# Block two's attention in a two-block layer kernel: where the softmax coefficients are applied, and which operand of p·v stands still

## The reference, cut to what matters

```python
s_c = jnp.einsum('bsgrd,bngd->bgrsn', qh, kc) - slopes * dist_c        # 15 compressed keys
p_c = masked_softmax(s_c, dist_c >= 0)
o_cmp = jnp.einsum('bgrsn,bngd->bsgrd', p_c, vc)
...
s = jnp.einsum('bgrqk,...', qb, kg) - slopes * dist                    # "selected", then "window"
pr = masked_softmax(s, valid)
o_slc = pr @ vg                                                        # o_win likewise
...
gates = jax.nn.sigmoid(gate).reshape(B, S, G, R, 3)
o = gates[..., 0:1] * o_cmp + gates[..., 1:2] * o_slc + gates[..., 2:3] * o_win
...
mixed = (g_a * (ya @ w_a2d) + g_b * (yb @ w_b2d)) @ w_o
```

## Time and profile before

| what | value |
|---|---|
| median of three runs | 1124.86 us |
| span of the profiled execution | 1122.6 us |
| PE busy | 1094.1 us (97%) |
| POOL busy | 902.3 us (80%) |
| ACT busy | 621.2 us (55%) |
| DVE busy | 495.1 us (44%) |
| mean granted clock of TensorE | 0.998 |

### The profile page before, as it was taken

How to read it: one execution, slowest core, us unless ns; L and a number is a source line. 1 busy time by engine, 2 the same in 40 slices (tenths; PEclk the granted TensorE clock), 3 DMA queues, 4 the chain that set the end, 5 groups by cost and what they waited for, 6 DMA issues and landing times.

```text
span 1122.6 us, 22288 instructions
## 1 busy us (share of the span) xinstructions
PE 1094.1 (97%) x8110; PEld 1023.2 (91%) x8110; DVE 495.1 (44%) x904; ACT 621.2 (55%) x1002; POOL 902.3 (80%) x695
## 2 busy tenths in 40 slices
PE   8999999999999999999999999999999999999997
PEld 7999998999998998999999899889999798999985
DVE  4422113202456554421126655774766256454463
ACT  4444444654667866544443775555666565555564
POOL 6999996898664596999999589577355898999985
PEclk9999999999999999999999999999999999999999
DMA  7866665666342454766665466335233565666652
GB/s 244 282 204 193 187 195 165 206 222 192 115 131 78 130 184 139 230 202 198 192 182 181 135 193 188 118 116 159 65 94 127 183 202 172 180 197 187 189 184 77
DMA packets 52774, 191.29 MB, mean 170 GB/s; under 512 B 5856, under 2 KB 6112, under 8 KB 52320
## 3 DMA queue, kind: packets, MB, share of 16 engines
q1 hardware_dynamic: 50688, 182.47, 52.6%
q10 hardware_dynamic: 2016, 7.81, 2.1%
HBM read 189.21 MB, written 1.05 MB: 169 GB/s over the span
## 4 chain that ended last, share of the span: by engine, by line
POOL 51%; issue 27%; PE 19%; ACT 1%; POOLq 1%; DVE 1%; DMA 1%; SPq 0%; DVEq 0%; ACTq 0%
POOL weights_low L533 51%; PE banks L575 10%; PE acc L575 8%; DMA ring<-in_stream 1%; POOLq L539 0%; ACT weights_high L1440 0%; POOLq L530 0%; ACT tmp L1686 0%; ACT tmp L1956 0%; PE acc L749 0%; PE banks L766 0%; DVE act_buf L2016 0%; DVE res L2162 0%; POOL stat L547 0%; DVE xs L2174 0%
## 5 line engine op out<-in xcount | busy, mean ns | idle before, releaser
L533 POOL TENSOR_TENSOR weights_low<-ring,weights_high 128x512 fp32r<-128x512 f32 x686 | 899.2, 1345 | 208.7 <-ACT weights_high L1440 206.5
L1440 ACT CAST weights_high<-ring 128x1024 fp32r<-128x1024 f32 x343 | 356.1, 1047 | 216.4 <-PE banks L575 132.0
L575 PE MATMUL banks<-xT_high,weights_high 128*128 128x256 f32 x1264 | 351.5, 278 | 1.2 <-POOL weights_low L533 1.1
L575 PE MATMUL banks<-xT_low,weights_high 128*128 128x256 f32 x1264 | 350.3, 277 | 0.0
L575 PE MATMUL banks<-xT_high,weights_low 128*128 128x256 f32 x1264 | 350.3, 277 | 0.0
L575 PEld LDWEIGHTS banks<-xT_high,weights_high 128*128 128x128 f32 x1264 | 237.4, 188 | 4.2 <-issue 1.5
L575 PEld LDWEIGHTS banks<-xT_low,weights_high 128*128 128x128 f32 x1264 | 237.7, 188 | 2.3
L575 PEld LDWEIGHTS banks<-xT_high,weights_low 128*128 128x128 f32 x1264 | 237.9, 188 | 0.0
L1991 DVE TENSOR_TENSOR hf<-act_buf,banks 128x256 f32<-128x256 f32 x40 | 16.8, 421 | 225.2 <-ACT act_buf L1466 211.0
L575 PE MATMUL acc<-xT_high,weights_high 128*128 128x256 f32 x408 | 108.8, 287 | 1.8 <-ACT xT_high L1539 1.0
L575 PE MATMUL acc<-weights_high,hT_high 128*128 128x512 f32 x264 | 104.0, 394 | 2.2 <-issue 1.6
(11 more groups left out here) (362 smaller groups left out, 1577.5 us busy)
## 6 DMA issues: line engine op xcount, KB each, us to landing
ring<-in_stream SPq DMA_DIRECT2D x343, 512.0 KB, 3.7
rows<-in_big_rows ACTq DMA_DIRECT2D x3, 1024.0 KB, 8.2
rows<-in_big_rows ACTq DMA_DIRECT2D x3, 512.0 KB, 4.0
cst<-in_consts ACTq DMA_DIRECT2D x3, 470.5 KB, 4.8
xs<-in_x_tm ACTq DMA_DIRECT2D x2, 512.0 KB, 7.3
out<-xs SPq DMA_DIRECT2D x4, 256.0 KB, 2.1
gates<-in_x_fm SPq DMA_DIRECT2D x2, 256.0 KB, 4.2
ring<-in_stream SPq DMA_DIRECT2D x2, 256.0 KB, 4.3
```

The source lines that it names most:

```text
L533: last = nc.gpsimd.tensor_tensor(wlo[:, slot, hs], ring[:, slot, hs], whi[:, slot, hs].bitcast(F32), ALU.subtract)
L575: ins = nc.tensor.matmul(o, lhsT, rhs, start=start, stop=stop, **kw)
L1440: nc.scalar.copy(whi[:, ch % RING, :], ring[:, ch % RING, :]).then_inc(S["hi_ready"], 1)
```

## The change

The coefficient (one over the row sum, times the gate) is now applied to the probabilities before they are transposed, for all three branches. The products can then be summed in PSUM, with features on partitions and tokens on columns, which is the layout `yT` needs. `both_tile(p)` is the half bank in which head pair p gathers compressed, selected and window products.

- `cmp_values` has v standing still (128 columns, two heads) and the probabilities moving; `both_values` has v of 64 columns standing still and 256 and 128 columns of probabilities moving, with m = 0 into the lower and m = 1 into the upper 64 partitions.
- DVE gets a multiply of 128x256 for each `tok` (signal `cmp_scaled`) and, in `both_coefs`, four multiplies in place on `both_prob` (128 and 256 columns, signal `both_scaled`). `both_coefs(h-1)` now stands ahead of `both_bias(h)`.
- `compressed_out`, `both_add`, `o2`, `turn_y(2)` and `turn_y(3)` are gone. `high_both` on ACT and `low_both` on DVE split a finished head pair (128x256) straight from PSUM. DVE's three multiplies on GDN's output move from rounds 1, 2, 3 to rounds 1, 3, 5.

```diff
+        def both_tile(p):
+
+            return acc[:, 2 + p % 2, T * (p // 2):T * (p // 2) + T]
...
                 for tok in range(2):
-                    pe.wait_ge(S["cmp_probs"], tok + 1)
+                    pe.wait_ge(S["cmp_scaled"], tok + 1)
...
                     pe.wait_ge(S["cmp_pt"], tok + 1)
-                    for g in range(2):
-                        last = nc.tensor.matmul(acc[:, 2 + tok, g * T:(g + 1) * T], cpT[:, tok, g * P:(g + 1) * P], bdv[:, g, :],
-                                                start=True, stop=True)
-                    last.then_inc(S["cmp_done"], 1)
+                    for p in range(4):
+                        g, heads = p // 2, slice(P * (p % 2), P * (p % 2) + P)
+                        mm(both_tile(p)[:, P * tok:P * tok + P], bdv[:, g, heads], cpT[:, tok, g * P:(g + 1) * P], tok == 0 and p < 2, False,
+                           skip_group_check=True)
...
-                src = og if k < 2 else o2
...
                     for tok in range(2):
-                        f = 2 * (k % 2) + kk
-                        last = nc.tensor.transpose(acc[:, (k + 2) % 4, (2 * kk + tok) * P:(2 * kk + tok + 1) * P],
-                                                   src[:, tok, f * P:(f + 1) * P], ident)
+                        f = 2 * k + kk
+                        last = nc.tensor.transpose(acc[:, k, (2 * kk + tok) * P:(2 * kk + tok + 1) * P],
+                                                   og[:, tok, f * P:(f + 1) * P], ident)
...
                 skip(f"both_t{e}")
-                pe.wait_ge(S["both_probs"], 4 * e + 4)
+                pe.wait_ge(S["both_scaled"], e + 1)
...
                 pe.wait_ge(S["both_pt"], e + 1)
-                if e >= 2:
-                    pe.wait_ge(S["both_out"], e - 1)
-                vc = P * (e % 2) + 64 * (e // 4)
-                for m in range(2):
-                    pT, o = both_pT[:, e % 2, m], acc[:, e % 2, P * m:P * m + P]
-                    mm(o[:, 0:64], pT[:, 0:P], sm[:, 0, vc:vc + 64], True, True)
-                    mm(o[:, 64:P], pT[:, P:2 * P], sm[:, 0, vc:vc + 64], True, False)
-                    last = mm(o[:, 64:P], pT[:, 2 * P:3 * P], sm[:, 1, vc:vc + 64], False, True)
+                p, kind = e // 2, e % 2
+                if p >= 2 and kind == 0:
+                    pe.wait_ge(S["yT_ready"], p - 1)
+                vc = P * kind + 64 * (e // 4)
+                two = [(both_tile(p)[64 * m:64 * m + 64], both_pT[:, kind, m]) for m in range(2)]
+                for o, pT in two:
+                    mm(o, sm[:, 0, vc:vc + 64], pT[:, 0:T], False, False, skip_group_check=True)
+                for o, pT in two:
+                    last = mm(o[:, P:T], sm[:, 1, vc:vc + 64], pT[:, T:3 * P], False, kind == 1, skip_group_check=True)
...
                     if h in (1, 2):
-                        pe.wait_ge(S["cmp_out"], h)
+                        pe.wait_ge(S["cmp_pt"], h)
...
                     if b == 0 and k % 2 == 0:
-                        pe.wait_ge(S["yT_ready"], k // 2 + 1)
+                        pe.wait_ge(S["yT_ready"], 2 + k // 2 + 1)
+                    if b == 1 and k >= 2:
+                        pe.wait_ge(S["yT_ready"], 2 + k + 1)
...
             done(mix_part(o[1], 0))
-            pe.wait_ge(S["both_out"], H2)
-            turn_y(2)
-            turn_y(3)
             mix_part(o[2], 0)
-            pe.wait_ge(S["yT_ready"], 4)
...
-            def high_y(k, order):
-                act.wait_ge(S["yT_turned"], order + 1)
-                nc.scalar.copy(yT[0][:, 2 * k:2 * k + 2, :].rearrange("p a t -> p (a t)"), acc[:, (k + 2) % 4, :]
+            def high_y(k):
+                act.wait_ge(S["yT_turned"], k + 1)
+                nc.scalar.copy(yT[0][:, 2 * k:2 * k + 2, :].rearrange("p a t -> p (a t)"), acc[:, k, :]
                                ).then_inc(S["yT_high"], 1)
+            def high_both(p):
+                wait_job(f"both_o{2 * p + 1}")
+                nc.scalar.copy(yT[0][:, 4 + p, :], both_tile(p)).then_inc(S["yT_high"], 1)
...
                     both_copy(h - 1)
+                if h in (4, 6):
+                    high_both(h // 2 - 2)
...
             both_exp(H2 - 1)
-            high_y(0, 0)
-            high_y(1, 1)
+            high_y(0)
+            high_y(1)
+            high_both(2)
...
             act.wait_ge(S["gmix_raw"], 16)
-            high_y(2, 2)
-            high_y(3, 3)
+            high_both(3)
...
                     link(v.tensor_scalar(cc, cc, c("rowvalid"), None, ALU.mult))
+                v.tensor_tensor(s3, s3, cc.unsqueeze(2).broadcast_to([P, H2, 32]), ALU.mult).then_inc(S["cmp_scaled"], 1)
...
-            def compressed_out(tok):
-                dve.wait_ge(S["cmp_done"], 10 + tok + 1)
-                cc = ccol[:, 24 * tok + 16:24 * tok + 24]
-                mark(v.tensor_tensor(o2[:, tok, :].rearrange("p (h d) -> p h d", h=H2), acc[:, 2 + tok, :].rearrange("p (h d) -> p h d", h=H2),
-                                     cc.unsqueeze(2).broadcast_to([P, H2, 64]), ALU.mult), "cmp_out", tok + 1)
-            def low_y(k, order):
-                dve.wait_ge(S["yT_high"], order + 1)
+            def low_y(k):
+                dve.wait_ge(S["yT_high"], 2 + k + 1)
                 hi, lo = (x[:, 2 * k:2 * k + 2, :].rearrange("p a t -> p (a t)") for x in yT)
-                low(lo, acc[:, (k + 2) % 4, :], hi).then_inc(S["yT_ready"], 1)
+                low(lo, acc[:, k, :], hi).then_inc(S["yT_ready"], 1)
+            def low_both(p):
+                dve.wait_ge(S["yT_high"], (1, 2, 5, 6)[p])
+                low(yT[1][:, 4 + p, :], both_tile(p), yT[0][:, 4 + p, :]).then_inc(S["yT_ready"], 1)
...
                 mark(v.tensor_tensor(pair, pair, sm[:, :, at:at + 4:3], ALU.mult), "both_coef", e + 1)
-            def both_add(e):
-                job_wait(dve, f"both_o{e}")
-                for m in range(2):
-                    for tok in range(2):
-                        at = P * m + 64 * tok
-                        d = o2[:, tok, 64 * (e // 2 * 2 + m):64 * (e // 2 * 2 + m) + 64]
-                        last = v.scalar_tensor_tensor(d, acc[:, e % 2, at:at + 64], coef2[:, e % 2, 2 * tok + m:2 * tok + m + 1],
-                                                      d, ALU.mult, ALU.add)
-                mark(last, "both_out", e + 1)
-            for h in range(H2 + 2):
+                for t, lo, hi in ((0, 0, P), (1, P, 3 * P)):
+                    for m in range(2):
+                        part = both_prob[:, e % 2, m, lo:hi]
+                        last = v.tensor_scalar(part, part, coef2[:, e % 2, 2 * t + m:2 * t + m + 1], None, ALU.mult)
+                last.then_inc(S["both_scaled"], 1)
+            for h in range(H2 + 1):
+                if h:
+                    both_coefs(h - 1)
...
                     both_bias(h)
-                if 1 <= h <= H2:
-                    both_coefs(h - 1)
+                if h in (5, 7):
+                    low_both((h - 5) // 2)
                 if h == H2:
-                    low_y(0, 0)
-                    low_y(1, 1)
-                if h >= 2:
-                    both_add(h - 2)
-                if h == 0:
-                    compressed_out(0)
-                    compressed_out(1)
-                elif h == 1:
+                    low_y(0)
+                    low_y(1)
+                if h == 1:
...
                     link(v.tensor_tensor(og8, og8, stat[:, 44:52].unsqueeze(2).broadcast_to([P, 8, P]), ALU.mult))
-                elif h == 2:
+                elif h == 3:
                     link(v.tensor_tensor(og8, og8, sr("gdn_norm", P).unsqueeze(1).broadcast_to([P, 8, P]), ALU.mult))
-                elif h == 3:
+                elif h == 5:
...
                     v.tensor_tensor(ogf, ogf, zs[:].rearrange("p a n -> p (a n)"), ALU.mult).then_inc(S["gdn_normed"], 1)
-            low_y(2, 2)
-            low_y(3, 3)
+            low_both(2)
+            low_both(3)
```

15 lines of the change are left out of this document (7 added, 8 removed).

## The result

The changed kernel takes 1132.26 us (median of four runs, 1129.15 to 1132.75), the kernel before 1125.22 beside it. The ratio is 1.006, with a 95% interval of 1.0047 to 1.0072: slower by 7 us, where +9.8 was forecast. The profiled execution has a span of 1130.3 us against 1122.6, so 7.7 us have to be found.

A forecast was written before the change was run, and what follows sets the result against it. PE was taken to bound the attention rounds, with the DVE and ACT chain as the new bound; 3.5 + 8.3 - 2.0 = +9.8 us gave a span of 1132.4 and a median of 1134.6, range 1123 to 1141.

The forecast's parts named there:

- What bounds the kernel: Attention rounds: PE, busy 10.00 of 10.00 us at full clock, so every PE step removed is worth its time.
- Part 1: Compressed branch: PE waits for DVE's multiplies, the second blocked by POOL; the next PE step comes +3.5 us later.
- Part 2: Attention rounds: p·v in four matmuls, heads side by side, costs 0.85 us instead of 1.38.
- The lower bound of 0.64: PE's p·v in a round: half of 768 columns at four passes and 2.4 GHz, 0.64 us at least.
- Part 3: Attention rounds: closed DVE and ACT chain, fourth multiply behind one POOL instruction, 6.1 us a round; +8.3 in all.
- second turn: Round 5: DVE reaches the coefficients 0.2 to 0.3 late, so two POOL turns are lost instead of one; +1.5 us.
- Part 4: Behind the attention: eight transposes and both waits go (1.6 us), p·v gives 0.4; -2.0 in all.
- Rival 1: Attention rounds: DVE keeps the port through four multiplies, or the fourth starts before POOL asks; 1124.6 to 1126.3, chance 0.25.
- Rivals 2 and 3: Rounds: p·v's column halves not running together, 1127 to 1131, chance 0.1; multiplies costing more, 1142 to 1144, chance 0.08.

The follow-up runs named there:

- the wide form: The changed kernel with two multiplies over both heads, the coefficient broadcast along the columns, in place of four, POOL not held: 1125.14 us, ratio 1.0005.

## Why the prediction was right, and where its terms were off

Slower was right, and by the mechanism that the runs found. The sum was 2 us too high: one term 1.2 too small, one 3.0 too large, and 0.5 came back where I had put nothing. That the total lies so close is in part luck, since the errors have opposite signs.

**What bounds the kernel.** PE was the bound and had no slack: confirmed. With the waits gone, PE's round is 5.24, as forecast (5.2).

**Part 1, +3.5 forecast, +4.7 measured.** The first half's wait (0.45 forecast, 0.48), the small product blocked by POOL's first instruction (0.87 long), the multiply by its second, its end at 795.3, 795.0 without the 0.3 of drift (795.15 forecast): each step came within 0.2 us of what was worked out. What was missing is the clock: I had costed transposes, state and values behind the wait at full speed. At 0.50 they took 1.3 to 1.4 more. In the profiles in which the clock stayed, the part comes to about 3.3. So the term for the wait was right and the one for the work behind it wrong.

On the port: the multiply takes 1.44 behind POOL and 0.43 with POOL held. By the Trainium skill, page "SBUF — State Buffer", section "SBUF: two separate sides", the port pair is locked for a whole instruction by whichever starts first, and these two rows agree. So does the wide form, where POOL comes second and is the one that waits.

**Part 2, p·v 0.85 forecast, 0.80 measured.** The value came from the scores' row, in the belief that two heads run side by side. One head alone at 0.79 bears that out: the second adds nothing. The Trainium skill, page "TensorE: Matmul & The Clock Gate", Part 3, "The mechanism", spoke against it: weight loads hidden only when the row group differs, by which I had estimated nearer 1.9. The traces don't bear that out. The lower bound of 0.64 wasn't reached. The transposes cost 0.75 in a stream where I kept 0.66 from before: 0.1 a round that I didn't see.

**Part 3, +8.3 forecast, +5.3 measured.** The chain is closed, and by what I said: with POOL held the rounds fall to PE's 5.24. Two terms were too large. First, the bias starts 2.50 behind the cast and not 2.75: the multiplies begin at 0.54 instead of 0.57, and behind POOL's first instruction (812.40 and 1.32) the last multiply needs 0.1, not the 0.4 that I had put there. That is 5.85 a round for 6.1, 1.5 us over the six rounds, and 0.25 once more at bias 7. Second, round 5 lost no second turn (1.5):

```profile
839.54 1.22 DVE L2640 TENSOR_TENSOR res<-res,zs 128x1024 f32<-128x1024 f32 x1
840.71 0.18 DVE L2612 RECIPROCAL coef<-den 128x4 f32<-128x4 f32 x1
```

The cast of that round starts at 840.58, and the coefficients at 840.71 are on time. Bias, maxima, split and product took 3.47 from the start of the bias (837.24) where I had summed 3.73: I had added full durations, and on DVE the next record starts up to 0.1 us before the one ahead ends (1.17 for the product's 1.22). The step was decided on 0.2 us, and that is the size of this error. The other way goes the end: ACT's copy of round 6 stands ahead of the exponentials of round 7, so that these start 1.94 behind bias 7 (848.91 to 850.85) and not 1.58, which takes 0.3 back. 1.75 and 1.5 less 0.3 are the 3.0 between forecast and trace.

**Part 4, -2.0 forecast, -2.0 measured.** The eight transposes and both waits went as said. That POOL wouldn't bind behind it held too, and was worth more than the nothing I gave it: about 0.5 came back.

**Rival 1** (PE as the bound, 1124.6 to 1126.3) is what the kernel becomes when POOL is held (1126.13) or when no fourth multiply is there to be caught (1125.14). Its condition was named rightly, that the last multiply starts before POOL asks, and the changed kernel misses it by 0.1 us (POOL starts 1.10 behind the cast, while the third is running; the fourth is recorded 1.20 behind it). **Rivals 2 and 3** fell: p·v is at 0.80, and the multiplies of 128 columns start 0.2 apart, so that the third is under way (812.23) when POOL asks (812.40).

One wait of the changed kernel I had not priced by itself: 3.29 us in round 7, where PE has no filler. It was in the sum, since that was counted to the last transposes. The clock fell there as well, which cost 0.2: the transposes of round 6 take 1.07 us for 0.88, ACT's copy waits for them, and the last transposes start 47.2 behind the first scores, against 47.05 in the one profile whose clock stayed (POOL held at the compressed branch).

## What to carry to other kernels

- A dependent series of short VectorE instructions beside a GpSimd stream can let a GpSimd instruction in at each of its gaps: merge it into one or two instructions, or hold GpSimd until it is done when its result isn't needed for some time. Either was worth 6 to 7 us here, for a delay of 0.3 to 0.6 us a round on GpSimd.
- When work is moved into a chain that several engines share, count the cycle with each order of the instructions, and in each the last turn by the program order of the engine that ends it; opening it at one engine may close it at the next.
- Put the cost of a wait on TensorE at its length, and as an upper bound add what the work behind it loses at half clock; or fill it. Here 0.9 us of work inside the wait went with 2.3 us less.
- Before you explain 1 or 2 us between two profiles by an edit, compare the granted clock at the places that the edit doesn't touch.

## What the runs showed of the hardware that I had not expected

- TensorE's granted clock fell to 0.50 for a little over 3 us behind idle times of 2.44 to 2.46 us in three of six profiles with the same instructions ahead, and cost 1.4 us each time. At 360 us it did so behind 1.87 to 1.98 us, in seven of thirteen.
- In p·v two heads in column halves cost 0.80 to 0.81 us together, 0.81 in the other order, and one head alone 0.79.
- DVE multiplied 768 columns in SBUF in 1.01 us with four products by a column and in 1.03 with two products by a broadcast operand: the form that looks slower is no slower.
